# A hybrid decoder step on one core: sample tile as a fifth chain beside the prompt tiles' inversion, its transposed inverse by transposes, modulation slots by contraction step

## Chip, cores and metric

The kernel runs on one core of one Trainium2 chip. The metric is the device time of one execution in microseconds (us). In the profile PE is TensorE's matmuls, PEld its weight loads, DVE is VectorE, ACT is ScalarE, POOL is GpSimd and SP is SyncE, which issues the weight loads.

## What is computed

Two decoder layers work on 256 prompt tokens and on 64 sample tokens (8 sequences of 8). Each layer has a token mixer with four gated-linear-attention heads and four gated-delta heads, then a feed-forward (dense in layer 0, 8 experts of which 2 are used in layer 1). Shift, scale and gate of every normalization come from the conditioning, by a product with `w_ada`. The part that the change touches, for the gated-delta heads, in the reference's words:

```python
m = jnp.where(strict, beta_h[..., :, None] * kk * lmask, 0.0)
t_inv = lax.linalg.triangular_solve(eye + m, eye, left_side=True, lower=True, unit_diagonal=True)
u = t_inv @ (v * beta);  w = t_inv @ (k * beta * exp(gam));  a_qk = (q @ k.T) * lmask
# per chunk, with the state s
v_new = uu - ww @ s
o = qd @ s + aa @ v_new
s = s * exp(gl) + kd.T @ v_new
# and for every block of w_ada
mod = cs @ w_ada[l] + b_ada[l]
```

Here a chunk is a whole tile. For the samples each sequence has a state of its own, read from memory and written back. All of it is fp32; the large weight products are split into a high and a low fp32r part and take three matmuls.

## The kernel before, in words

**Tiles.** `TILES` (line 65) are prompt tokens 0 to 127 (tile 0), 128 to 255 (tile 1) and the 64 sample tokens (tile 2). A layer is: input projection (29 units of 128 outputs), mixing stage, out-projection (8 units), feed-forward. In the mixing stage five engines have each their own program, and the order of the work is written out by hand on each; semaphores counted by name and value (`after`, `PER_LAYER`) tie them together. There is no planner.

**Mixing stage, TensorE's order** (from line 910 on): scores and values of the linear-attention heads (`gla_scores`, `gla_values`) and, for the delta heads, `turn` (transposes of q, k, v to token rows, and the decay sums along rows), `turn_back` (normalized q, k transposed back) and `products` (k k and k q), for tile 0 and then tile 1. Then `invert((0, 1), ...)`, then `keys`, `new_values`, `outputs` for tile 0 and tile 1, and only then `turn`, `turn_back`, `products`, `invert`, `keys`, `new_values`, `outputs` for tile 2. VectorE's `normalize` and `strict` make the matrices of a tile (lines 1841 to 1892), ScalarE's `squares_qk`, `masks`, `turned_back`, `row_decay` stand between.

**Inversion** (lines 806, 1388 and 1894). The unit triangular matrix of a head is inverted by doubling blocks: 7 levels for a prompt tile, 3 for the sample tile, whose sequences have 8 tokens. `DM` is the matrix, `DMB` its part that belongs to a level (VectorE's `masked`, line 1839), `DT` and `DU` the inverse and its transpose so far. At each level TensorE computes DY from DMB and DU, ScalarE copies DY from PSUM, TensorE computes DT-times-DY and DY-times-DT, and VectorE subtracts one from DU (line 1914) and the other from DT (line 1913). At level 0 the first product is one with the identity. Two heads of a tile form a chain with a PSUM bank of its own; tiles 0 and 1 together make four chains whose steps alternate, tile 2 later makes two. Beside the levels stand the sample tokens of the linear-attention heads (`samples_beside`): on TensorE `gla_sample_values` at levels 1 and 2 and `gla_sample_state` at levels 3 to 6, on VectorE `spread` (line 1808), `decayed` (line 1813) and `added` (line 1819). `gla_sample_state(2)` waits for the first `added`, as they use the same two banks.

**Buffers.** The parts of tiles 0 and 1 have a set of nine buffers each (`DSET`, in the area of the split weights); tile 2 uses tile 0's set again, after tile 0 and 1 are done. `settled` holds TensorE back until VectorE and ScalarE have read a tile's results.

**Modulation.** A group `x` of `ada` is 16 output blocks: 8 contraction steps `k` of four matmuls, which write 32 rows each of one bank. SyncE loads it into 8 of the ring's 8 slots (1 MB each), in load order with all other weights; a slot is loaded again when its user has counted it done (`used`). Slot g of a half holds output quarter g for four steps k, so step 0 waits for four slots, and they come free together after step 3. In each layer three groups are computed in the mixing stage, split over TensorE's queue by `ada(x, ...)`. `ada_rows` (ScalarE), `ada_turn` (TensorE, line 648) and `ada_add` (VectorE, line 1661) finish one.

**Tail.** After `outputs(2)`: VectorE squares the heads (`heads_square`, line 1622), TensorE sums them (`heads_sum`), VectorE and ScalarE take the reciprocal root (`heads_root`, lines 1627 and 1577 to 1579, `rsqrt_seed`), TensorE spreads it over the partitions (`heads_spread`), VectorE scales (`heads_scale`, line 1639), and ScalarE and VectorE split the result into `hh` and `hl`, which the out-projection reads block by block. Weights are split by ScalarE (`high.to`, line 413) and VectorE (`low.to`, line 418).

All matmuls of the mixing stage go through the helper `mm`, line 594; all activations through line 1227.

## Time and profile before

| | |
|---|---|
| runs | 2052.96, 2054.32, 2056.16 us; median 2054.32 |
| profiled execution | 2056.35 us, its span 2054.2 us |
| PE / PEld busy | 1913.9 us (93%) / 1575.9 us (77%) |
| DVE / ACT / POOL busy | 1466.7 us (71%) / 1092.8 us (53%) / 12.6 us (1%) |
| mean granted TensorE clock | 0.956 of 2.4 GHz |
| memory read / written | 494.88 MB / 8.72 MB, 245 GB/s over the span |

The span is the time from the first to the last instruction, and the execution's own time is 2.15 us longer. Busy shares are means over stages with different limits: the experts of layer 1 (from about 960 us on) hold most of TensorE's time. The clock has two levels, 1.2 and 2.4 GHz; a value between 0.5 and 1 for a stretch says for how much of it the full one was granted. In the timeline a row merges instructions of one kind that follow each other: its first number is the start, the second the time from the first start to the last end.

### The profile page before, as it was taken

The page shows a single profiled execution, that of the slowest core. Times are in us where ns is not written, and L with a number is a line of the kernel's source. Part 1 is how long each engine was busy: PE and PEld are TensorE (multiplying, and loading weights), DVE is VectorE, ACT ScalarE, POOL GpSimd, SP SyncE. Part 2 cuts the span into 40 slices and gives each one's busy share as a digit, 9 for nine tenths or more (in the row PEclk, how much of TensorE's full clock was granted, in tenths as well). Part 3 has the DMA queues.
Part 4 walks back from the last instruction along what each step waited for, and adds up shares of the span by engine and source line. Part 5 has one row for each costly group of instructions (what it writes and reads, how often), then busy time and mean ns, then how long its engine had stood idle before and what let it go on. Part 6 is the DMA issues. An engine that isn't in the chain of part 4 may idle for free.

```text
span 2054.2 us, 25480 instructions
## 1 busy us (share of the span) xinstructions
PE 1913.9 (93%) x10376; PEld 1575.9 (77%) x10376; DVE 1466.7 (71%) x1831; ACT 1092.8 (53%) x1105; POOL 12.6 (1%) x27
## 2 busy tenths in 40 slices
PE   6997889899999989896999999999999999999995
PEld 3994757899989957565778788787787877878783
DVE  3847746654448668466688888888887888878885
ACT  3744223333337542233667676666766766767672
POOL 0000000000000000000000000000000000000000
PEclk9998999999999989797899999999999999999998
DMA  9444264343352442552699899898898998989980
GB/s 383 145 147 183 87 251 159 138 155 112 127 195 103 147 158 102 222 204 83 255 338 360 321 342 349 322 361 322 342 352 322 357 334 333 350 319 358 335 340 27
DMA packets 70616, 505.30 MB, mean 246 GB/s; under 512 B 8064, under 2 KB 8224, under 8 KB 11872
## 3 DMA queue, kind: packets, MB, share of 16 engines
q1 hardware_dynamic: 68112, 488.29, 63.4%
q0 software_dynamic: 2384, 15.34, 2.0%
q8 instruction: 84, 1.38, 0.3%
q14 instruction: 36, 0.29, 0.0%
HBM read 494.88 MB, written 8.72 MB: 245 GB/s over the span
## 4 chain that ended last, share of the span: by engine, by line
issue 55%; PE 31%; DVE 10%; ACT 2%; DMA 1%; SPq 0%; POOL 0%; DVEq 0%; ACTq 0%; POOLq 0%
PE bank L594 30%; DVE wlo L418 1%; DVE work L1687 1%; ACT L1227 1%; DMA raw<-in_ada 1%; ACT work L1227 1%; DVE work L1688 1%; DMA raw<-in_w_in 0%; DVE wscr L1839 0%; ACT wscr L1227 0%; DVE hT L1601 0%; DVE work L1782 0%; DVE wscr L1908 0%; DVE rt L1577 0%; DVE rs L1579 0%
## 5 line engine op out<-in xcount | busy, mean ns | idle before, releaser
L418 DVE TENSOR_TENSOR wlo<-raw,whi 128x2048 fp32r<-128x2048 f32 (+1 forms) x412 | 920.0, 2262 | 212.0 <-ACT whi L413 210.3
L413 ACT ACTIVATE whi<-raw 128x2048 fp32r<-128x2048 f32 (+1 forms) x412 | 761.6, 1889 | 87.4 <-PE bank L594 74.9
L594 PE MATMUL bank<-whi,hg_high 128*128 128x512 f32 x896 | 369.2, 412 | 1.5 <-DVE hg_low L2104 1.5
L594 PE MATMUL bank<-whi,hg_low 128*128 128x512 f32 x896 | 355.2, 396 | 0.0
L594 PE MATMUL bank<-wlo,hg_high 128*128 128x512 f32 x896 | 355.1, 396 | 0.0
L594 PE MATMUL bank<-hh,whi 128*128 128x320 f32 x944 | 299.7, 317 | 23.0 <-DVE hl L1609 18.6
L594 PE MATMUL bank<-hh,wlo 128*128 128x320 f32 x944 | 294.3, 312 | 0.0
L594 PE MATMUL bank<-hl,whi 128*128 128x320 f32 x944 | 294.2, 312 | 0.0
L1227 ACT ACTIVATE work<-bank 128x512 f32<-128x512 f32 (+2 forms) x209 | 97.3, 487 | 274.2 <-PE bank L594 250.6
L594 PEld LDWEIGHTS bank<-hh,whi 128*128 128x128 f32 x944 | 180.7, 191 | 30.6 <-issue 23.7
L594 PEld LDWEIGHTS bank<-whi,hg_high 128*128 128x128 f32 x896 | 169.1, 189 | 43.2 <-issue 4.4
L594 PEld LDWEIGHTS bank<-whi,hg_low 128*128 128x128 f32 x896 | 169.1, 189 | 41.1
L594 PEld LDWEIGHTS bank<-wlo,hg_high 128*128 128x128 f32 x896 | 169.4, 189 | 38.2
L594 PE MATMUL bank<-whi,act_high 128*128 128x512 f32 x448 | 185.2, 413 | 1.5 <-DVE act_low L2107 1.5
L594 PEld LDWEIGHTS bank<-hh,wlo 128*128 128x128 f32 x944 | 181.0, 192 | 0.8
L594 PEld LDWEIGHTS bank<-hl,whi 128*128 128x128 f32 x944 | 180.4, 191 | 0.0
L594 PE MATMUL bank<-wlo,act_high 128*128 128x512 f32 x448 | 177.2, 395 | 0.0
L594 PE MATMUL bank<-whi,act_low 128*128 128x512 f32 x448 | 177.1, 395 | 0.0
L594 PE MATMUL bank<-work 128*128 128x128 f32 (+9 forms) x704 | 112.6, 332 | 7.8 <-DVE work L1782 4.1
L1227 ACT ACTIVATE wscr<-bank 128x256 f32<-128x256 f32 (+3 forms) x86 | 36.9, 436 | 142.8 <-PE bank L594 112.1
L594 PEld LDWEIGHTS bank<-wscr 128*128 128x128 f32 (+2 forms) x752 | 87.9, 194 | 25.1 <-issue 15.0
L594 PE MATMUL bank<-wscr 128*128 128x128 f32 (+3 forms) x752 | 97.5, 284 | 8.5 <-DVE wscr L1908 5.8
(243 smaller groups left out, 1895.9 us busy)
## 6 DMA issues: line engine op xcount, KB each, us to landing
raw<-in_moe SPq DMA_DIRECT2D x336, 1024.0 KB, 4.8
raw<-in_ada SPq DMA_DIRECT2D x56, 1024.0 KB, 7.0
raw<-in_w_in SPq DMA_DIRECT2D x30, 1024.0 KB, 4.9
raw<-in_gu SPq DMA_DIRECT2D x22, 1024.0 KB, 4.9
raw<-in_down SPq DMA_DIRECT2D x16, 704.0 KB, 4.0
raw<-in_w_out SPq DMA_DIRECT2D x8, 1024.0 KB, 7.9
work<-in_s_gdn POOLq DMA_DIRECT2D x2, 2048.0 KB, 9.5
out_gdn_s<-work POOLq DMA_DIRECT2D x2, 2048.0 KB, 7.4
```

What stands on the lines that cost most here:

```text
L413: ac.activation(whi[:, part(n), 0:width(n)], raw[:, n % SLOTS, 0:width(n)], ACT.Copy).then_inc(S("w_high"), 1)
L418: ve.tensor_tensor(wlo[:, n % SLOTS, 0:width(n)], raw[:, n % SLOTS, 0:width(n)], whi[:, part(n), 0:width(n)], ALU.subtract).then_inc(S("w_ ...
L594: return pe.matmul(out, lhsT, rhs, start=start, stop=stop, **k)
L1227: return ac.activation(out, in_, func, **k)
L1687: go(stt(yp, XP[:, s, j:j + TP], wc[:, c, j:j + 1], yp, ALU.mult, ALU.add))
L1688: do(stt(ys, xs[:, :, j:j + LSEQ], wc[:, c, j:j + 1], ys, ALU.mult, ALU.add))
```

## The change

- Tile 2 gets a buffer set of its own (made of free parts of the two areas and of buffers that tiles 0 and 1 have done with), and goes through `turn`, `turn_back`, `products`, `normalize` and `strict` before the inversion. It is inverted as a fifth chain, of all four heads, in levels 2 to 4 of the one `invert`.
- `DT` is no longer updated. From a chain's level 2 on TensorE transposes DU (`pe.transpose`, against the identity) into the first half of the bank, computes DY into the second half, and ScalarE copies both halves in one activation (`DTY`). VectorE subtracts from DU alone. The product with the identity at level 0 becomes a transpose.
- `gla_sample_values` and the score masking of tile 2 move before the inversion, `gla_sample_state` to levels 1 to 4, and with them `spread`, `decayed` and `added`. The end of modulation group x (`ada_rows`, `ada_turn`, `ada_add`), all of group x + 1's products and the head sums of the linear-attention heads move into the inversion.
- Behind the inversion the tiles' `keys`, `new_values` and `outputs` interleave; `settled` becomes single waits. `sample_rows` goes before `second_state`. The new values get buffers `DVN`.
- The second of the first two out-projection splits goes behind the sample outputs on ScalarE, and behind `low_parts` on VectorE. The root's table load goes before the copy of the modulation rows, and the third modulation turn goes behind the spread.
- A modulation slot holds one contraction step of all four quarters: 2 KB pieces from memory, a wait, a use count and a release per step.

The diff, cut to its core (indentation shortened; bodies that it replaces are the functions printed above):

```diff
 DSP = v3(w(512, NH * NK), NH)
-DSET = [[wscr[:, at + 512 * i:at + 512 * (i + 1)] for i in range(9)] for at in (PARTS * HALF - 9 * 512, 0)]
-DY = DSET[0][7]
+DSET = [[wscr[:, at + 512 * i:at + 512 * (i + 1)] for i in (0, 1, 2, 3, 4, 5, 7, 6, 8)] for at in (PARTS * HALF - 9 * 512, 0)]
+DTY = [v3(wscr[:, at + 512 * 5:at + 512 * 7], 2) for at in (PARTS * HALF - 9 * 512, 0)]
+AT2, DU2 = R1 + 4736 - 256, DSET[1][8]
+DT2, DY2, DX2 = w(AT2, 512), w(AT2 + 512, 256), w(R1, 256)
+DSET.append([wscr[:, 9 * 512:10 * 512], wscr[:, 10 * 512:11 * 512], DSET[0][8], DT2[:, 256:], DU2[:, 256:], DT2, DU2, DY2, DX2])
+DTY.append(v3(w(AT2, 1024), 2))
+DVN = [DSET[0][7], DSET[1][7], DSET[0][5]]
+DY = DVN[2]
 D01, D34 = w(0, 512), w(2 * TL, 512)
 WQ_AT = (WORK, WORK + NSEQ * P)
 NB, XB = (B[0], B[4], B[2], B[3]), (B[5], B[6], B[7])
-IBANK = (NB[0:2], NB[2:4], NB[0:2])
+IBANK = (NB[0:2], NB[2:4], XB[1:2])
 SBANK = ((B[3], B[4]), (B[1], B[2]))
 STATE_AT = (0, 1, 3, 4)
...
     if x is not None:
-        return S("ada_mm"), 2 * x + (n - AT_ADA[x]) // 4 + 1
+        return S("ada_mm"), n + 1 - AT_ADA[x] + KD * x
...
+def chains(v):
+    yield from ((i, hs, v) for i in range(2) for hs in range(2))
+    if 2 <= v < 2 + LEVELS[2]:
+        yield 2, 0, v - 2
+def chain(i, hs):
+    nt = TILES[i][1]
+    heads = (2 * hs, 2 * hs + 1) if i < 2 else range(NH)
+    return nt, heads, slice(heads[0] * nt, (heads[-1] + 1) * nt), IBANK[i][hs]
+LEVELS = (7, 7, 3)
+STEPS = [x for v in range(7) for x in chains(v)]
...
             sp.wait_ge(*used(n - SLOTS))
-        sp.dma_start(raw[:, n % SLOTS, 0:width(n)], src).then_inc(landed[n % SLOTS], 16)
+        dst = raw[:, n % SLOTS, 0:width(n)]
+        sp.dma_start(dst if group_of(n) is None else v3(dst, 4), src).then_inc(landed[n % SLOTS], 16)
     def load_ada(x, b):
-        for g in range(4):
-            load(AT_ADA[x] + 4 * b + g, A["ada"][2 * (4 * x + g) + b, :, :])
+        for k in range(4):
+            chunks = A["ada"][8 * x + b:8 * x + 8:2, :, k * CH:(k + 1) * CH]
+            load(AT_ADA[x] + 4 * b + k, chunks.rearrange("g p c -> p g c"))
     load_ada(0, 0)
...
         for k in ks:
-            b = k // 4
+            n = AT_ADA[x] + k
             if k == 0 and x:
                 pe.wait_ge(S("ada_done"), x)
+            pe.wait_ge(landed[n % SLOTS], 16 * (n // SLOTS + 1))
             for g in range(4):
-                n = AT_ADA[x] + 4 * b + g
-                if k % 4 == 0:
-                    pe.wait_ge(landed[n % SLOTS], 16 * (n // SLOTS + 1))
                 ins = mm(ABANK[32 * g:32 * g + 32, :], small[:, k * NC_:k * NC_ + 32],
-                         raw[:, n % SLOTS, (k % 4) * CH:(k % 4 + 1) * CH], k == 0, k == KD - 1)
-            if k % 4 == 3:
-                ins.then_inc(S("ada_mm"), 1)
+                         raw[:, n % SLOTS, g * CH:(g + 1) * CH], k == 0, k == KD - 1)
+            ins.then_inc(S("ada_mm"), 1)
     def ada_turn(x):
...
+        def invert(beside):
+            after(pe, "dat", l, 3)
+            after(pe, "drowe", l, 3)
+            for v in range(LEVELS[0]):
+                for i, hs, x in chains(v):
+                    nt, heads, _, bank = chain(i, hs)
+                    DMB, DU = DSET[i][4], DSET[i][6]
+                    after(pe, "dmb", l, AT_MASK[i, hs, x])
+                    if x:
+                        after(pe, "dtu", l, AT_LEVEL[i, hs, x - 1])
+                    elif i == 2:
+                        after(pe, "gla_o", l, 3)
+                    for h in heads if x > 1 else ():
+                        o = (h - heads[0]) * nt
+                        pe.transpose(bank[0:nt, o:o + nt], DU[0:nt, h * nt:(h + 1) * nt], ident[0:nt, 0:nt])
+                    for h in heads:
+                        c = slice(h * nt, (h + 1) * nt)
+                        o = 256 + (h - heads[0]) * nt
+                        if x:
+                            ins = mm(bank[0:nt, o:o + nt], DMB[0:nt, c], DU[0:nt, c])
+                        else:
+                            ins = pe.transpose(bank[0:nt, o:o + nt], DMB[0:nt, c], ident[0:nt, 0:nt])
+                    ins.then_inc(S("dy_mm"), 1)
+                for i, hs, x in chains(v):
+                    if x == 0:
+                        continue
+                    nt, heads, _, bank = chain(i, hs)
+                    DT, DY = DSET[i][5], DSET[i][7]
+                    after(pe, "dy", l, AT_UPDATE[i, hs, x])
+                    for h in heads:
+                        c = slice(h * nt, (h + 1) * nt)
+                        o = (h - heads[0]) * nt
+                        ins = mm(bank[0:nt, o:o + nt], DT[0:nt, c], DY[0:nt, c])
+                    ins.then_inc(S("dtu_mm"), 1)
                 beside(v)
...
+            after(pe, "dtu", l, len(STEPS))
...
                 if i == 2:
-                    if h == 0:
-                        ada(x + 2, 4, 5)
                     after(pe, "dwm", l, h + 1)
...
+        def beside(v):
+            if 0 < v < 5:
+                gla_sample_state(v - 1)
+            if v == 1:
+                ada_turn(x)
+            if v > 1:
+                ada(x + 1, *((0,), (1, 2), (3, 4), (5, 6), (7,))[v - 2])
+            if v == 5:
+                after(pe, "gla_sstate", l, 2)
+                heads_sum(("heads", 2 * l + 1), QK)
         gla_scores(0)
...
+        ada(x, 5)
+        turn(2)
+        gla_sample_values(0)
+        gla_sample_values(1)
+        ada(x, 6)
+        turn_back(2)
         ada(x, 7)
-        invert((0, 1), samples_beside)
-        ada_turn(x)
+        products(2)
+        invert(beside)
         keys(0)
-        heads_sum(("heads", 2 * l + 1), QK)
         new_values(0)
-        ada(x + 1, 0, 1)
+        keys(1)
         outputs(0)
-        ada(x + 1, 2)
-        settled(0)
-        keys(1)
+        ada_turn(x + 1)
         heads_spread(("heads", 2 * l + 1))
+        after(pe, "gdn_state", l, 1)
         new_values(1)
-        ada(x + 1, 3, 4)
+        ada(x + 2, 0)
+        keys(2)
+        ada(x + 2, 1)
+        after(pe, "do", l, 1)
         outputs(1)
-        ada(x + 1, 5)
-        settled(1)
-        turn(2)
-        ada(x + 1, 6, 7)
-        turn_back(2)
-        products(2)
-        ada_turn(x + 1)
-        invert((2,), lambda v: None)
-        ada(x + 2, 0, 1, 2, 3)
-        keys(2)
+        ada(x + 2, 2, 3)
         new_values(2)
+        ada(x + 2, 4)
+        after(pe, "do", l, 2)
         outputs(2)
-        ada(x + 2, 6, 7)
+        ada(x + 2, 5)
         after(pe, "do", l, 3)
         heads_sum(("heads", 2 * l + 2), w(4 * TL, TL))
+        ada(x + 2, 6, 7)
+        heads_spread(("heads", 2 * l + 2))
         ada_turn(x + 2)
-        heads_spread(("heads", 2 * l + 2))
...
-            nt, DM, DMB = TILES[i][1], DSET[i % 2][3], DSET[i % 2][4]
+            nt, (DM, DMB) = TILES[i][1], DSET[i][3:5] if i < 2 else DSET[i][5:7]
             for b, dst in ((0, DM), (1, DMB)):
                 after(ac, "dtr", l, 3 * i + b + 1)
-                if i == 2 and b == 0:
-                    after(ac, "gdn_state", l, i)
+                if i == 2 and b == 1:
+                    after(ac, "dqd", l, i)
                 act(dst[0:nt, :], NB[b][0:nt, :], ACT.Square).then_inc(S("dsq"), 1)
             rsqrt_seed(("qk", 3 * l + i + 1), rv8[0:nt, :], rs8[0:nt, :])
...
+        def invert(beside):
+            for v in range(LEVELS[0]):
+                for i, hs, x in chains(v):
+                    if x == 0:
+                        continue
+                    nt, _, c, bank = chain(i, hs)
+                    after(ac, "dy_mm", l, AT_LEVEL[i, hs, x])
+                    if x > 1:
+                        ins = act(DTY[i][0:nt, :, c], v3(bank, 2)[0:nt, :, 0:256], ACT.Copy)
+                    else:
+                        ins = act(DSET[i][7][0:nt, c], bank[0:nt, 256:512], ACT.Copy)
+                    ins.then_inc(S("dy"), 1)
                 beside(v)
...
             act(DMB[:, 0:n4], NB[0][:, 0:n4], ACT.Copy, scale=-1.0).then_inc(S("dw"), 1)
         def new_values(i):
             after(ac, "dvn_mm", l, i + 1)
-            act(DSET[i % 2][7], NB[1][:, :], ACT.Copy).then_inc(S("dvn"), 1)
+            act(DVN[i], NB[1][:, :], ACT.Copy).then_inc(S("dvn"), 1)
         def outputs(i):
...
+        squares_qk(2)
+        gla_result(2)
+        masks(2)
+        turned_back(2)
+        row_decay(2)
+        invert(lambda v: ada_rows(x) if v == 0 else None)
+        rsqrt_seed(("heads", 2 * l + 1))
         keys(0)
         new_values(0)
-        rsqrt_seed(("heads", 2 * l + 1))
+        ada_rows(x + 1)
+        keys(1)
         outputs(0)
-        keys(1)
         new_values(1)
+        keys(2)
         outputs(1)
-        squares_qk(2)
-        masks(2)
-        ada_rows(x + 1)
-        turned_back(2)
-        row_decay(2)
-        invert((2,), lambda v: None)
-        keys(2)
-        high.to(AT_OUT[l] + 1)
+        after(ac, "ds_mm", l, 2)
+        high.to(AT_OUT[l])
         new_values(2)
         outputs(2)
+        high.to(AT_OUT[l] + 1)
         after(ac, "gla_fin", l, 1)
         for k in range(GH):
             act(hh[:, k, :], hT[:, k, :], ACT.Copy).then_inc(S("hh"), 1)
+        rsqrt_seed(("heads", 2 * l + 2))
         ada_rows(x + 2)
-        rsqrt_seed(("heads", 2 * l + 2))
...
+            if i == 2:
                 do(cp(v3(gEL[:, :], 4), v3(DX[:, 0:n4], 4)[:, :, LSEQ - 1:TS:LSEQ]))
...
+                    (nt, heads, c, bank), DU = chain(i, hs), DSET[i][6]
+                    if x + 1 < LEVELS[i]:
+                        masked(i, hs, x + 1)
+                    if x == 0:
+                        nh = len(heads)
+                        after(ve, "dy_mm", l, AT_LEVEL[i, hs, 0])
+                        do(tt(v3(DU[0:nt, c], nh), mid(ident[0:nt, 0:nt], nh),
+                              v3(bank[0:nt, 256:512], nh), ALU.subtract), "dtu")
+                        continue
+                    after(ve, "dtu_mm", l, AT_UPDATE[i, hs, x])
+                    do(tt(DU[0:nt, c], DU[0:nt, c], bank[0:nt, 0:256], ALU.subtract), "dtu")
                 beside(v)
...
             for h in range(NH):
-                ins = stt(DSP[:, h, :], DSP[:, h, :], gEL[:, 4 + h:5 + h], NB[3][:, h * P:(h + 1) * P], ALU.mult, ALU.add)
+                ins = stt(DSP[:, h, :], DSP[:, h, :], gX[:, h:h + 1], NB[3][:, h * P:(h + 1) * P], ALU.mult, ALU.add)
                 go(ins) if h < NH - 1 else do(ins, "gdn_state")
         def sample_rows():
-            t0, DMB, n4 = TP, DSET[0][4], 4 * TS
+            t0, DMB, n4 = TP, DSET[2][4], 4 * TS
             after(ve, "gla_out", l, 48)
...
+        o1, tag1 = hT[:, 0:GH, :], ("heads", 2 * l + 1)
+        def beside(v):
+            if v == 3:
                 added(0)
...
+            if v < 4:
+                spread(v)
+            if v == 1:
+                ada_add(x)
+            if v in (2, 3):
+                decayed(v - 2)
+            if v == 5:
                 added(1)
+                heads_square(tag1, o1, QK)
         arguments(1)
         gla_scored(0)
...
         gla_carried(1)
         operands(2)
         strict(1)
...
+        gla_scored(2)
         normalize(2)
         strict(2)
+        after(ve, "gla_o", l, 3)
+        invert(beside)
+        heads_root(tag1)
+        heads_gate(o1, G1, col(f"glan{l}"))
+        first_state()
         ada_add(x + 1)
...
+        heads_scale(tag1, o1, "gla_fin", False)
         sample_rows()
...
+        second_state()
+        low.to(AT_OUT[l])
         after(ve, "do", l, 3)
         def sample_values(h):
...
         o2, tag2 = hT[:, GH:, :], ("heads", 2 * l + 2)
         heads_square(tag2, o2, w(4 * TL, TL))
         low_parts(3 * l + 1, "hl_out", range(GH))
```

## Rows read from the trace of the kernel before

**Rows 1.** Stretches: us, busy PE, PEld, DVE, ACT, POOL; granted clock, DMA share, GB/s.
```profile
153.10:199.70 46.60, 36.11 (x297) 22.25 (x298) 35.51 (x94) 22.15 (x42) 1.62 (x3) 0.85 0.40 153
199.70:242.70 43.00, 40.48 (x329) 36.46 (x330) 35.33 (x82) 9.61 (x25) 0.54 (x1) 1.00 0.24 100
242.70:311.10 68.40, 55.59 (x412) 36.22 (x412) 31.02 (x72) 16.33 (x28) 1.60 (x3) 0.90 0.57 227
311.10:325.90 14.80, 11.43 (x52) 6.71 (x51) 9.53 (x20) 5.96 (x13) 0.00 (x0) 0.67 0.68 261
729.20:902.30 173.10, 145.66 (x1082) 103.92 (x1082) 111.08 (x266) 53.42 (x107) 3.52 (x7) 0.86 0.45 178
```

**Rows 2.** Timeline of the inversion: sample values, a sample-state product, a level of products.
```profile
207.57 2.30 PE L594 MATMUL bank<-work 128*128 128x64 f32 x20
...
222.85 1.07 PE L594 MATMUL bank<-work 32*64 32x512 f32 x4
...
223.85 5.43 PEld L594 LDWEIGHTS bank<-wscr 128*128 128x128 f32 x48 [0.81 <-issue]
```

**Rows 3.** Timeline: the twelve transposes of one turn.
```profile
177.85 1.29 PEld L779 LDWEIGHTS bank<-cf,work 128*128 128x128 f32 x12 [2.04 <-DVE work L1879]
```

**Rows 4.** Groups by form, 199.7 to 242.7: count | busy us, mean ns | idle before.
```profile
L1839 DVE TENSOR_TENSOR wscr<-wscr,cb 128x256 f32<-128x256 f32 x24 | 10.2, 425 | 1.8 <-PE bank L594 1.0
...
L1227 ACT ACTIVATE wscr<-bank 128x256 f32<-128x256 f32 x24 | 9.2, 384 | 28.0 <-PE bank L594 27.3
L1913 DVE TENSOR_TENSOR wscr<-wscr,bank 128x256 f32<-128x256 f32 x20 | 8.4, 421 | 4.7 <-PE bank L594 4.1
...
L1813 DVE TENSOR_TENSOR work<-work,gla_expend 128x1024 f32<-128x1024 f32 x2 | 2.5, 1226 | 0.1
...
L1819 DVE TENSOR_TENSOR work<-work,bank 128x512 f32<-128x512 f32 x2 | 1.3, 684 | 0.0
```

**Rows 5.** Timeline after the inversion: spread, two modulation steps, sample values and outputs.
```profile
260.41 2.33 PE L594 MATMUL bank<-rs,cf 128*128 128x320 f32 x10
...
264.45 1.92 PE L594 MATMUL bank<-raw,small 128*32 128x512 f32 x16
...
297.91 2.05 PE L594 MATMUL bank<-work 128*128 128x128 f32 x16
...
307.38 0.60 ACT L1227 ACTIVATE wscr<-bank 128x512 f32<-128x512 f32 x1 [3.06 <-PE bank L594]
308.03 0.29 PEld L594 LDWEIGHTS bank<-work,wscr 64*128 64x128 f32 x2 [0.93 <-ACT wscr L1227]
```

**Rows 6.** Timeline of the tail, and the two low splits ahead of it.
```profile
302.91 4.49 DVE L418 TENSOR_TENSOR wlo<-raw,whi 128x2048 fp32r<-128x2048 f32 x2
...
311.09 3.41 PE L594 MATMUL bank<-raw,small 128*32 128x512 f32 x16
...
315.19 1.28 ACT L1227 ACT_TABLE_LOAD   x1
...
316.59 0.45 ACT L1227 ACTIVATE rs<-rv 128x320 f32<-128x320 f32 x1
...
318.94 4.63 PE L594 MATMUL bank<-rs,cf 128*128 128x320 f32 x10 [3.06 <-DVE rt L1629]
```

**Rows 7.** Timeline: first and last of tile 2's preparation on VectorE, 24 instructions.
```profile
272.32 0.68 DVE L1848 TENSOR_REDUCE rv<-wscr 64x4 f32<-64x512 f32 x1
...
281.91 0.17 DVE L1892 COPY g_expend<-wscr 128x32 f32<-128x32 f32 x1
```

**Rows 8.** Two stretches, columns as in rows 1.
```profile
273.00:282.00 9.00, 5.40 (x53) 3.09 (x52) 8.45 (x23) 3.85 (x8) 0.00 (x0) 1.00 1.01 411
282.00:293.00 11.00, 8.89 (x60) 5.61 (x64) 5.64 (x17) 1.08 (x4) 0.00 (x0) 0.56 0.54 229
```

**Rows 9.** Timeline of the start: first projection split and modulation add.
```profile
32.67 1.91 ACT L413 ACTIVATE whi<-raw 128x2048 fp32r<-128x2048 f32 x1 [4.54 <-DMA raw<-in_w_in]
...
36.89 0.30 DVE L1661 TENSOR_TENSOR mod<-bank,small 128x144 f32<-128x144 f32 x1
```

168 lines of the change are left out of this document (40 added, 128 removed).

## Prediction

> **What bounds the kernel now.** I first cut the first layer's mixing stage into stretches by busy time [rows 1]. The reader should see 172.8 us from 153.1 to 325.9, with TensorE busy 143.6 (36.1 + 40.5 + 55.6 + 11.4) and its granted clock under 1.00 in three of the four stretches. The second layer repeats it (173.1 us). So this stage, twice, is where TensorE waits or runs at 1.2 GHz. Outside it the change touches only the load and use order of the modulation weights. Inside it the bound changes hands. From 153.1 to 199.7 VectorE prepares the two prompt tiles. From 199.7 to 242.7 their four inversion chains keep TensorE busy 40.5 of 43.0 us, at full clock. From 242.7 to 311.1 one tile after another goes round TensorE, ScalarE and VectorE, and 12.8 us are idle on TensorE. 311.1 to 325.9 is the tail, a chain through all three engines before the out-projection can use its fifth input block.
>
> **Prices.** In the inversion a 128-wide product is two instructions of 0.113 us (5.43 / 48), so 0.23 [rows 2]; a transpose is one of 0.107 us (1.29 / 12) [rows 3]. Four heads make 0.9 or 0.45. VectorE pays 0.42 for a mask and 0.42 for a subtraction, ScalarE 0.38 for a copy of two heads, and the sample work beside costs VectorE 1.23 (decay) and 1.28 (two rows of state add) [rows 4]. The sample-state product costs TensorE 1.07 and one contraction step of the modulation 0.96 at full clock (1.92 / 2) and 1.7 at half (3.41 / 2) [rows 2, 5, 6].
>
> **Term 1, inversion starts later: +11.7 us a layer.** Tile 2's preparation moves ahead of the inversion. On VectorE it runs from 272.32 to 282.08, so 9.8 us [rows 7]. The sample scores' masking (a memset and two small products, estimate 0.8, by the 0.28 to 0.42 of other 64- and 128-row operations of a few hundred columns) leaves level 0 and joins it. TensorE must now do turn, both sample-value calls (2.3 each [rows 2]), three modulation steps and turn-back in that time, and ScalarE does a table load and one result copy before the masks. By my count the key products come 1.9 late for VectorE. Against that, the two modulation steps that stood in front of turn-back of tile 1 are gone, which gives 0.6 (tile 1's products then hang on the operands of the sample scores). Sum 9.8 + 0.8 + 1.9 - 0.6 = 11.9, less 0.2 for two wide masks in place of four narrow ones.
>
> **Term 2, inversion itself: +6.0 and +3.0.** The second operand's update, two products (0.45) and one VectorE subtraction (0.42) a chain and level, becomes two transposes (0.21) and a wider copy. That copy is not in the trace: bounds are 0.38 (no more than one copy) and 0.77 (two), I take 0.6, and ScalarE, busy 9.6 of 43, hides either. A chain then costs TensorE 0.45 + 0.21 + 0.45 = 1.11 and VectorE 0.9, four chains 4.4 and 3.6. Level 0's products with the identity become transposes too, under VectorE's masks. On top lie tile 2's chain in levels 2 to 4 (64-wide, 12 instructions a level or fewer, 0.3, 1.0 and 1.3), a state product in levels 1 to 4 and eight modulation steps of the next group. By level, in TensorE's time: 0 and 1 together 7.5 (VectorE paces level 0, then state product and turn); level 2, 4.4 + 0.3 + 1.0 + 0.9 = 6.6; level 3, 5.4, then a **new wait**: the third state product may not overwrite its bank before VectorE's first state add, which now stands in the same level behind five chains' subtractions, 3.7 us late, then 1.0 + 1.8, so 11.9; level 4, 4.4 + 1.3 + 1.0 + 1.8 = 8.5; level 5, 4.4 + 1.8, then a **second wait** of 3.2 us, because the head sums stand in TensorE's queue before level 6 and need VectorE's second state add (1.28) and the squares (1.5), then 0.7, so 10.1; level 6, 4.4. Sum 49.0 against 43.0. The clock adds: level 0 and tile 2's products are thin work for TensorE, and in the trace the stretch 273 to 282, busy 5.4 of 9.0, is followed by one at 0.56 [rows 8]. I count half clock over part of levels 1 and 2, +3.0 (bounds 0 and 7, the work of those levels).
>
> The Trainium skill speaks against this part: TensorE: Matmul & The Clock Gate, Part 4: PE-mode transpose, says that transposes do not count as TensorE work for keeping the clock up. This trace does not separate it; it is taken up as a rival below.
>
> **Term 3, from the end of the inversion to the end of the sample outputs: -37.4.** Now 68.4 us [rows 1], of which tile 2's preparation and inversion (270.5 to 289.3) and eight of its fourteen modulation steps leave, some of them at half clock. What remains for TensorE at full clock: keys of three tiles and two tiles' values (1.0 + 3 x 0.88 + 1.75), outputs 0 and 1 (1.75 + 2.65), the turn 0.45, the spread 2.3 [rows 5], sample values 307.38 - 297.91 = 9.4 and sample outputs 311.09 - 308.03 = 3.1 [rows 5, 6], six modulation steps at 0.86 start to start, 5.2, and 0.8 waiting for a ScalarE copy. Sum 31.0. The ScalarE copies that TensorE waited for lie under modulation steps and the next tile's keys; without that cover each costs some 0.8. The sample rows on VectorE (two memsets, 2.4) are ready before the sample values begin, since TensorE needs 14 us to get there. The buffers for the new values and the decay column moved to a free tile take waits away that nothing hung on; I price them, the dropped settle calls and the shifted state copy at 0. The state load (2 MB) is issued after the fourth state product, over 15 us before its use.
>
> **Term 4, the tail: +2.2.** Today 14.8 us. The second out-projection split leaves its place under the sample values for a place behind the last outputs: 1.9 on ScalarE before the copies of the head blocks and 2.24 on VectorE before the root [rows 6]. ScalarE's reciprocal-root table, today loaded from 315.19 on, with the root at 316.59, is loaded before it is needed; the variance is there at about 315.7, which gives 0.9; and the modulation steps no longer delay the head sums, 1.2. The turn of the third modulation group now stands behind the spread, and VectorE's scale waits for it, 1.3. I leave the spread at half clock (4.63 against 2.33 [rows 5, 6]), since TensorE has 5 us of nothing before it. Sum 1.9 + 2.2 - 0.9 - 1.2 + 1.3, less 1.1 where the two splits overlap: 2.2.
>
> **Term 5, modulation slots by contraction step: 0.** At the start TensorE can multiply when one slot is there, not four, and after the last load one step remains instead of four. But ScalarE's copy of the rows stands behind the split of the first projection weights, which waited for its load until 32.67 and ended at 34.58, and the modulation add follows VectorE's half of that split at 36.89 [rows 9]. Both hang on the load order, which stays. Each load now fetches pieces of 2 KB in place of 8 KB. No row shows it; below 0 is excluded by the splits, above I allow +5 at the start (8 MB at a quarter less speed) and take 0. In the layers the loads have slack.
>
> **Sum.** 11.7 + 6.0 + 3.0 - 37.4 + 2.2 = -14.5 a layer, -29 in all. What follows the stage (feed-forward, experts) only shifts. The profiled execution took 2056.35 us (span 2054.2 and 2.15 around it): 2027.3. The median shown is 2.0 lower, so **2025**. A measurement of this kernel can tell about 0.2%, 4 us, from no change.
>
> **Rivals.**
> *Waits shorter, clock kept (2015).* TensorE's full clock through levels 1 and 2 and the spread, and the two new waits half as long: 3.0 + 2.3 + 3.5 less than forecast, some -23 a layer, 2009; half of that gives 2015 to 2017. For it: 204 to 243 ran at 1.00. Against: the idle is placed as in the stretches that fell. Chance 0.20.
> *The chains bind on VectorE or on hand-overs (2039).* My sum passes over some 60 hand-overs between engines in the inversion; at 0.1 us each and a late sample-value call it loses 7 more a layer. Chance 0.12.
> *Half clock through the inversion (slower).* Place: levels 2 to 6. They hold 33 us of TensorE work a layer; at 1.2 GHz each of these costs one more, less the 7 of new waits that they fill and the 3 counted: +23 a layer, so 2025 + 46 = 2071. It decides from 14.5 us of such work a layer on. For it: TensorE's work is thinner per level and broken by two waits of over 3 us; a stretch at 5.4 of 9.0 busy lost the clock [rows 8]. Against: levels 3 to 5 are 70 to 100% busy between the waits, as 199.7 to 242.7 was. Chance 0.05, and 0.05 for half of it (2048).
> The skill's rule on transposes, named above, would make this rival likelier than the rows do, since a fifth of each level's TensorE time is transposes.
> *Loads of 2 KB pieces slow (2045).* Twice the time for the first 8 loads adds some 20 us at the start. Nothing in the trace speaks for it. Chance 0.03.
> My own forecast, 2015 to 2037: 0.55.
>
> **How the numbers follow.** Range 2008 to 2043: it holds the forecast, the faster rival and the hand-over one, and leaves out 0.13 and some of the edges. Faster by over 0.2%: all but the slower rival and a little of the mild ones, 0.93; slower 0.05; the same 0.02.
>
> **What would show it.** VectorE's first level-0 mask of the last chain set near 211 in place of 199.7; the last level's products ending near 263; no product reading the second operand as moving data in the inversion; TensorE idle over 3 us before the third state product and before the first head sums; sample outputs ending near 294; the out-projection's fifth block near 311 in place of 325.9. I am wrong if the inversion takes over 60 us, if the granted clock there is near 0.5, or if the first projection product starts later than at 41.

## The result and the profile after

The changed kernel takes **2042.7 us** (median of 4 runs, 2042.4 to 2043.3) against 2055.2 us of the kernel before on the same chip (4 runs, 2053.0 to 2056.7). The ratio is 0.9938, 95% interval 0.9925 to 0.9950. So it is faster, by 12.5 us and not by the 29 forecast. The profiled execution took 2043.25 us, its span 2041.5. PE busy is 1903.1 us (before 1913.9), DVE 1450.5 (1466.7), ACT 1101.1 (1092.8).

The stretches of layer 0 that answer to [rows 1] (columns as there; the last row is the stage of layer 1):

```profile
154.13:216.19 62.06, 50.46 (x370) 34.09 (x371) 45.18 (x118) 28.25 (x53) 1.43 (x3) 0.75 0.50 170
216.19:270.40 54.21, 47.33 (x362) 33.99 (x360) 33.01 (x68) 15.51 (x27) 1.60 (x3) 0.91 0.47 163
270.40:302.48 32.08, 31.39 (x240) 23.92 (x239) 13.39 (x31) 7.75 (x13) 0.55 (x1) 1.00 0.66 250
302.48:319.10 16.62, 11.23 (x59) 6.01 (x58) 11.59 (x21) 6.31 (x13) 0.00 (x0) 0.79 0.59 223
722.10:887.20 165.10, 139.16 (x1027) 97.52 (x1027) 103.26 (x237) 57.91 (x105) 3.57 (x7) 0.87 0.53 188
```

The preparation became 62.1 us (from 46.1, counted from VectorE's first operation of the stage), the inversion 54.2 (43.0), what follows it 32.1 (68.4), the tail 16.6 (14.8). The stage of layer 1 went from 173.1 to 165.1. A gain of some 8 us a layer stands where 14.5 were forecast, and it is the first two stretches that are too long. Their granted clocks, 0.75 and 0.91, say where to look. TensorE's timeline of the changed kernel through tile 2's preparation:

```profile
202.07 5.51 PE L610 MATMUL bank<-work 128*128 128x64 f32 x40
207.51 1.94 PE L610 MATMUL bank<-raw,small 128*32 128x512 f32 x8
209.38 0.69 PE L806 MATMUL bank<-cf,work 64*128 64x64 f32 x4
209.86 0.63 PE L806 MATMUL bank<-cf,wscr 64*128 64x64 f32 x4
210.42 1.93 PE L610 MATMUL bank<-raw,small 128*32 128x512 f32 x8
212.28 1.97 PE L610 MATMUL bank<-work 128*64 128x64 f32 x16
```

and VectorE's, of the same stretch:

```profile
208.32 0.68 DVE L1886 TENSOR_TENSOR wscr<-bank,g_beta 64x512 f32<-64x512 f32 x1
213.51 0.42 DVE L1895 TENSOR_TENSOR work<-bank,work 64x256 f32<-64x256 f32 x1 [4.51 <-PE bank L610]
```

The two modulation steps around turn-back take 1.94 and 1.93 us, the time of half clock (1.06 at full), and so do the key products (1.97, against 1.15 in the kernel before). VectorE waits 4.5 us for them. Three stretches with their granted clocks (columns as in rows 1), the first at tile 1's key products, the others at tile 2's preparation:

```profile
191.00:198.00 7.00, 6.10 (x34) 4.86 (x38) 3.03 (x10) 0.97 (x2) 1.09 (x2) 0.50 0.30 94
200.00:205.00 5.00, 4.94 (x44) 4.61 (x42) 4.63 (x13) 2.88 (x5) 0.00 (x0) 1.00 0.67 213
206.00:214.00 8.00, 8.00 (x48) 4.52 (x47) 3.39 (x7) 3.16 (x6) 0.00 (x0) 0.50 0.40 135
```

The kernel before has 0.98 where the first row has 0.50:

```profile
191.00:198.00 7.00, 5.37 (x50) 3.77 (x47) 4.02 (x11) 2.51 (x6) 1.08 (x2) 0.98 0.30 101
```

The third row deserves a second look: TensorE was busy 4.94 of the 5 us in the second row and went on without a pause, and still the clock is at half from 206 on. No idle gap stands in front of this fall, and no run shows what causes it. TensorE's timeline further on, at the two waits that the prediction placed:

```profile
236.33 0.67 PE L610 MATMUL bank<-work 64*64 64x64 f32 x8
240.70 1.97 PE L610 MATMUL bank<-work 32*64 32x512 f32 x4 [3.69 <-DVE work L1838]
242.60 3.64 PE L610 MATMUL bank<-raw,small 128*32 128x512 f32 x16
...
265.13 0.75 PE L610 MATMUL bank<-work,cf 128*32 128x320 f32 x8 [3.07 <-DVE work L1641]
```

Both are there, 3.7 and 3.1 us long (forecast 3.7 and 3.2). Behind the first the clock is at half: the state product takes 1.97 instead of the 1.07 of [rows 2], two modulation steps 3.64 instead of 1.92. Behind the second it stays full. The tail, whose rows answer to [rows 6]:

```profile
306.84 2.28 DVE L424 TENSOR_TENSOR wlo<-raw,whi 128x2048 fp32r<-128x2048 f32 x1
309.05 0.48 DVE L1646 TENSOR_SCALAR rv<-bank 128x320 f32<-128x320 f32 x1
...
311.92 3.86 PE L610 MATMUL bank<-rs,cf 128*128 128x320 f32 x10 [3.17 <-DVE rt L1648]
```

The first row is VectorE's half of the second out-projection split. It stands in front of the variance (the second row), which the root and then TensorE's spread (the third) wait for.

**Given back behind the layers.** When the out-projection of layer 1 reaches its fifth block, the changed kernel is 15.5 us ahead (887.16 against 902.64), and at the last scatter product still 15.05 (2006.38 against 2021.43). Another 2.3 us go in one place, VectorE's first operation after the experts. The kernel before, and then the changed one:

```profile
2029.00 0.48 DVE L1644 SCALAR_TENSOR_TENSOR xT<-hT,mod,xT 128x256 f32<-128x256 f32 x1 [1.54 <-issue]
```

```profile
2016.26 0.48 DVE L1663 SCALAR_TENSOR_TENSOR xT<-hT,mod,xT 128x256 f32<-128x256 f32 x1 [3.85 <-issue]
```

Nothing in the data holds it (the last scatter add has ended 3.85 us earlier, and "issue" is named), and the DMA queues carry nothing but instruction packets in this time. It is where VectorE's program jumps from the experts to what follows them.

### The profile page after: what moved, and what is told of

Its sections match the earlier page's. It is cut to its first block, busy times and chain, and to the rows that moved or that the text cites. A ratio compares the mean times of both kernels' runs of the same rounds, so it can differ in the third digit from the quotient of the medians.

```text
span 2041.5 us, 25178 instructions
## 1 busy us (share of the span) xinstructions
PE 1903.1 (93%) x10264; PEld 1566.4 (77%) x10264; DVE 1450.5 (71%) x1771; ACT 1101.1 (54%) x1101; POOL 12.7 (1%) x27
## 4 chain that ended last, share of the span: by engine, by line
issue 56%; PE 30%; DVE 11%; ACT 2%; SPq 1%; DMA 1%; POOL 0%; DVEq 0%; ACTq 0%; POOLq 0%
PE bank L610 29%; DVE wlo L424 2%; DVE work L1706 1%; SPq L524 1%; DMA raw<-in_w_in 1%; ACT L1241 1%; DVE wscr L1858 1%; PE bank L834 1%; DVE work L1707 1%; ACT work L1241 1%; DVE wscr L1930 0%; ACT whi L419 0%; DVE hT L1620 0%; DVE hl L1628 0%; DVE work L1838 0%
## 5 line engine op out<-in xcount | busy, mean ns | idle before, releaser
L1241 ACT ACTIVATE work<-bank 128x512 f32<-128x512 f32 (+3 forms) x217 | 101.3, 487 | 277.4 <-PE bank L610 247.9
L610 PE MATMUL bank<-work 128*128 128x128 f32 (+10 forms) x736 | 123.1, 344 | 13.4 <-DVE work L1838 7.4
L610 PEld LDWEIGHTS bank<-work 128*128 128x128 f32 (+4 forms) x736 | 83.6, 188 | 38.5 <-issue 19.7
L1241 ACT ACTIVATE wscr<-bank 128x512 f32<-128x512 f32 (+2 forms) x74 | 41.5, 567 | 132.7 <-PE bank L610 107.9
L610 PEld LDWEIGHTS bank<-whi,act_high 128*128 128x128 f32 x448 | 84.3, 188 | 24.9 <-issue 4.3
## 6 DMA issues: line engine op xcount, KB each, us to landing
work<-in_s_gdn POOLq DMA_DIRECT2D x2, 2048.0 KB, 12.6
out_gdn_s<-work POOLq DMA_DIRECT2D x2, 2048.0 KB, 7.4
```

The source lines that it names most:

```text
L610: return pe.matmul(out, lhsT, rhs, start=start, stop=stop, **k)
L1241: return ac.activation(out, in_, func, **k)
```

## The experiments

All edits are against the changed kernel unless said otherwise. The runs stem from several chips, on which the kernel before took 2054.4 to 2055.9 us, and their medians are compared with the 2043.4 of e0_after. Beside the medians I use one length from each trace, from VectorE's first operation of the mixing stage of layer 0 to that of layer 1 (the row that waits 13.5 us for ScalarE). It leaves out the start of the kernel, which scattered: in these traces the stage of layer 0 begins anywhere between 151.0 and 156.0. **Layer length**: before 575.6 us, changed kernel 568.0 and, in its second trace (e0_after), 567.3, to which the other lengths are compared.

**e0_after**, no edit.

> The changed kernel again, as the base for the others of this chip: 2042 to 2044 us in every theory. Two theories on the last 2.3 us (the start of the final residual on VectorE follows the last scatter 3.85 us later in the changed kernel, 1.54 in the kernel before, with 'issue' as the releaser and only instruction packets in the DMA queues): if it belongs to where the code lies, it is 3.8 again here; if it is chance, it scatters between 1.5 and 4.

Measured: 2043.4 us (2042.7 to 2044.5), the wait again 3.83. It belongs to the program. In this trace tile 2's key products ran at full clock (1.15 us) and VectorE still waited 4.17 for them, since the sample value calls (5.80) and the first modulation step (1.94) ahead of them did not.

**e1_add0**, the wait in level 3.

```diff
-                    if v == 3:
-                        added(0)
                     if v < 4:
                         spread(v)
...
                         decayed(v - 2)
+                    if v == 2:
+                        added(0)
```

> VectorE's first sample state add goes to the end of level 2, one level ahead of TensorE's third state product. Theory A (the wait of 3.7 us in level 3 is on the path and it also costs the clock behind it): the wait goes, the state product and two modulation steps behind it run at full clock (2.8 instead of 5.6), VectorE pays its 1.28 in level 2 instead: 4 to 5 us a layer, 2033 to 2035. Theory B (VectorE paces the levels anyway, the wait only shows it): the wait turns up in front of level 3's products and the time stays within 1 us a layer, 2041 to 2043.

Measured: 2035.0 us (2031.2 to 2036.6), layer length 561.4. Theory A. The same 12 us in the repeated changed kernel and in this one (columns as in rows 1):

```profile
237.00:249.00 12.00, 8.31 (x47) 3.50 (x47) 6.83 (x13) 0.48 (x1) 0.54 (x1) 0.72 0.27 91
```

```profile
237.00:249.00 12.00, 12.00 (x107) 7.92 (x100) 7.29 (x16) 3.23 (x6) 0.00 (x0) 1.00 0.55 187
```

The hole is closed, and the clock stays full. (The stage began 2.9 us earlier in the second trace, so the two windows do not hold quite the same work.) A wait of 3.7 us had cost 4.2 a layer by the medians and 5.9 by the layer length, whose trace is of the fastest of the four runs.

**e2_sums**, the wait before the head sums.

```diff
-                    if v == 5:
+                    if v == 6:
                         after(pe, "gla_sstate", l, 2)
                         heads_sum(("heads", 2 * l + 1), QK)
...
-                    if v == 5:
+                    if v == 4:
                         added(1)
+                    if v == 5:
                         heads_square(tag1, o1, QK)
```

> The head sums of the linear-attention heads go from ahead of level 6 to behind it on TensorE, and VectorE's second state add from level 5 to level 4. Theory A (the 3.1 us in which TensorE waits before the head sums are on the path): level 6 starts at once, its copies and products run under VectorE's squares, 2.5 to 3 us a layer less, 2037 to 2038. Theory B (level 6 has to wait for VectorE's level 5 anyway): under 1 us a layer, 2041 to 2043.

Measured: 2037.9 us (2036.5 to 2038.5), layer length 565.4. Theory A, 2.8 us a layer by the medians, 2.0 by the layer length. The clock had stayed full behind this wait, and it cost no more than its length.

**e7_tail**, the splits.

```diff
-                high.to(AT_OUT[l])
+                high.to(AT_OUT[l] + 1)
                 new_values(2)
                 outputs(2)
-                high.to(AT_OUT[l] + 1)
...
-                low.to(AT_OUT[l])
+                low.to(AT_OUT[l] + 1)
                 after(ve, "do", l, 3)
...
-                low.to(AT_OUT[l] + 1)
                 heads_root(tag2)
```

> Both out-projection splits stand again ahead of the sample outputs, on ScalarE before the new values of tile 2 and on VectorE before its wait for the outputs, both of which have over 5 us of idle time there. Theory A (VectorE's split of 2.28 us is on the path from the head sums to the root): the root starts 2.2 us earlier a layer, 2038 to 2040. Theory B (the split fills VectorE's wait for the head sums, which come late by the two modulation steps): under 0.5 us a layer, 2042 to 2044.

Measured: 2034.1 us (2033.7 to 2035.6): 9.3 us less, twice what Theory A gave. The timeline of its tail:

```profile
304.16 3.16 PE L610 MATMUL bank<-raw,small 128*32 128x512 f32 x16
304.66 0.48 DVE L1645 TENSOR_SCALAR rv<-bank 128x320 f32<-128x320 f32 x1
...
307.54 2.43 PE L610 MATMUL bank<-rs,cf 128*128 128x320 f32 x10 [0.22 <-DVE rt L1647]
```

The root starts right behind the head sums, which is the 2.3 us. And TensorE comes to the spread from the modulation steps without a pause, 0.22 us in place of 3.17, so that the spread takes 2.43 us and not 3.86. The two make 3.7 us a layer; the layer length is 564.3, 3.0 less, and the median gives 4.6.

**e4_fill** tests that second half by itself.

```diff
                 ada(x + 2, 6, 7)
+                for _ in range(12):
+                    mm(NB[0][:, 0:P], ident, ident)
                 heads_spread(("heads", 2 * l + 2))
```

> Twelve idle products of ident with ident (2.8 us at full clock), which compute nothing that is used, stand between the last two modulation steps and the spread of the tail, where TensorE has 3.2 us of idle time. Theory A (the spread takes 3.87 instead of some 2.3 us because the engine stood idle in front of it): the spread falls to 2.3 to 2.6, and as much of the time: 1 to 1.6 us a layer, 2040 to 2042. Theory B (the low clock there is the late effect of the gap from 304.8 to 305.9 or of the mixed work before): the spread stays at 3.9 and the time the same, 2043.

Measured: 2040.5 us (2039.4 to 2041.3). The tail of its trace:

```profile
308.02 2.94 PE L610 MATMUL bank<-cf 128*128 128x128 f32 x24
312.91 2.43 PE L610 MATMUL bank<-rs,cf 128*128 128x320 f32 x10 [1.94 <-DVE rt L1650]
```

Products that compute nothing make the work behind them faster, by 1.4 us a layer here, as much as the median fell. Theory A. In front of the spread stand 1.9 us of idle time here, 3.2 in the changed kernel. The head sums and modulation steps ahead of the fill happened to run at full clock in this trace. They did so in e1_add0 and e2_sums too, where without a fill 4.8 us of idle time follow and the spread takes 4.03 and 4.00, so it is the fill that helps.

**e6_notr**, the transposes undone.

```diff
-                            for h in heads if x > 1 else ():
...
-                                pe.transpose(bank[0:nt, o:o + nt], DU[0:nt, h * nt:(h + 1) * nt], ident[0:nt, 0:nt])
...
                                 ins = mm(bank[0:nt, o:o + nt], DT[0:nt, c], DY[0:nt, c])
+                            for h in heads if x < LEVELS[i] - 1 else ():
...
+                                ins = mm(bank[0:nt, o:o + nt], DY[0:nt, c], DT[0:nt, c])
...
+                            if x < LEVELS[i] - 1:
+                                go(tt(DT[0:nt, c], DT[0:nt, c], bank[0:nt, 256:512], ALU.subtract))
                             do(tt(DU[0:nt, c], DU[0:nt, c], bank[0:nt, 0:256], ALU.subtract), "dtu")
```

> The transposes of levels 2 to 6 are undone: the second operand is updated again by a product and a VectorE subtraction, all else stays. Theory A (prices by instruction): TensorE pays 21 chain updates of 0.45 and saves 22 sets of transposes of 0.21, VectorE pays 21 subtractions of 0.42, of which some fills its idle time: inversion 4.5 to 8 us longer a layer, 2051 to 2059. Theory B (transposes cost the clock, as TensorE: Matmul & The Clock Gate of the Trainium skill has it): the stretch at 0.50 in level 3 and the low clock at the head of the inversion go, worth 3 or more, and the net is 1.5 to 5 us a layer, 2045 to 2053, with a granted clock of 1.00 from level 1 to the end.

Measured: 2054.1 us (2051.8 to 2057.5, 11 runs), ratio to before 0.9994 (0.9985 to 1.0003), layer length 575.9. Theory A. That is the layer of the kernel before: **without the transposes the rest of the change, tile 2's chain beside the others included, brings nothing**. Whether the transposes would bring as much without the rest, no run shows. TensorE's timeline in its level 3 and before its head sums:

```profile
244.91 1.97 PE L610 MATMUL bank<-work 32*64 32x512 f32 x4 [3.54 <-DVE work L1836]
246.81 3.64 PE L610 MATMUL bank<-raw,small 128*32 128x512 f32 x16
...
270.79 1.14 PE L610 MATMUL bank<-work,cf 128*32 128x320 f32 x8 [3.06 <-DVE work L1639]
```

Wait and half clock are there without these transposes (those of level 0 stay), and the head sums, which took 0.75 in the changed kernel, run mostly at half clock (1.14). The granted clock of its inversion is 0.89 (216.4 to 276.0) where the changed kernel has 0.91. So these runs show no part of the clock's fall that is owed to the transposes of levels 2 to 6; the rule of the Trainium skill that the prediction names (TensorE: Matmul & The Clock Gate, Part 4: PE-mode transpose) would have had it rise.

**e3b_prep and e3c_prep**, the order of tile 2's preparation.

```diff
                 turn(2)
                 gla_sample_values(0)
-                gla_sample_values(1)
-                ada(x, 6)
                 turn_back(2)
-                ada(x, 7)
                 products(2)
+                gla_sample_values(1)
+                ada(x, 6)
                 invert(beside)
```

(cut: also step 7 beside level 0, ScalarE's result copy behind the row decay, and VectorE's wait for it in level 5)

> The preparation of tile 2 gets another order on TensorE: turn, first sample value call, turn back, key products, second sample value call, modulation step 6; step 7 goes beside level 0; ScalarE's result copy goes behind the row decay, and VectorE's wait for it to level 5. Theory A (the 4.5 us in which VectorE waits for tile 2's key products come from what stands ahead of turn-back and products in TensorE's queue, not from their own length): VectorE's wait falls under 1 us, and the inversion starts 3 to 4 us earlier a layer, 2035 to 2037. Theory B (the late stretch at half clock is what delays it, whatever the order): the wait falls by less than 2 us, and what stood there is paid at level 0, 2041 to 2044.

```diff
-                ada(x, 5)
                 turn(2)
                 gla_sample_values(0)
+                ada(x, 5)
                 gla_sample_values(1)
-                ada(x, 6)
                 turn_back(2)
-                ada(x, 7)
                 products(2)
+                ada(x, 6, 7)
```

> The preparation of tile 2 again, after the other order brought nothing: modulation step 5 goes between the two sample value calls, steps 6 and 7 behind the key products, all ahead of the inversion as in the changed kernel. Theory A (a modulation step at half clock in front of turn-back and one in front of the products make VectorE wait; behind the products they fall into TensorE's wait for the last decay): VectorE's wait of 4.5 us falls to 1 or 2 and the inversion starts 2 to 3 us earlier, 2037 to 2040. Theory B (the stretch at half clock from the sample values on sets when the inversion can start, in whatever order): the inversion starts within 1 us of where it did, 2042 to 2045.

Measured: 2048.0 (2045.3 to 2048.6) and 2050.4 us (2048.3 to 2054.6), layer lengths 572.1 and 574.7. Both made it worse, which neither theory had. TensorE's timeline of e3b_prep:

```profile
207.48 6.35 PE L610 MATMUL bank<-work 128*64 128x64 f32 x36 [0.47 <-ACT work L1242]
213.76 1.94 PE L610 MATMUL bank<-raw,small 128*32 128x512 f32 x8
215.63 1.97 PE L841 MATMUL bank<-cf,wscr 128*128 128x128 f32 x8
```

VectorE's wait for tile 2's products is gone (0.52 us), but TensorE, at half clock from 205 on, is not free for level 0 before 215.6: the second sample value call, in the first row with the products, now takes some 4.4 us where it takes 2.3 at full clock. VectorE then waits 5.07 us for level 0. In e3c_prep a gap of 1.57 us opens before the turn, which with the second sample value call runs at half clock (2.74 for 12 transposes, 4.45 for the call); the late call also holds up ScalarE's masks, and VectorE waits 7.05 us. In the changed kernel, with step 5 in front of the turn and both calls behind it, the turn (1.47) and most of the two calls (5.51 for both) ran at full clock.

**e5_slots**, the modulation slots as before (the diff's four edits on slots and use counts taken back).

> The modulation slots are undone alone: a slot holds one output quarter for four contraction steps again, is fetched in pieces of 8 KB and comes free with three others after step 3. Theory A (this part changes nothing but the 0.5 us of later issues at the start): within 1.5 us of the changed kernel, 2042 to 2045, its first projection split 0.5 us earlier. Theory B (a slot that comes free after each step is what lets the loads keep up with the modulation steps packed into the inversion): TensorE waits for modulation weights in the inversion or behind it, 3 us or more a layer, over 2048.

Measured: 2041.7 us (2039.5 to 2044.4), layer length 568.4, no wait of TensorE for a load in either layer's inversion or tail; the first projection split at 32.76, 0.43 earlier than in the changed kernel. Theory A. Runs that scatter by 5 can't tell 0 from 1.7 us, but the starts of all the traces together can: the first projection product stands between 39.9 and 41.1 us in the four with the slots as before (the kernel before, this one, c4, c6; mean 40.7) and between 41.3 and 43.4 in the twelve with the new ones (mean 42.1). So the new slots cost some 1.4 us, at the start alone.

**e9_shift**, code moved by 42 VectorE instructions.

```diff
-            ve.memset(gAB[:, :], 0.0)
+            for c in range(24):
+                ve.memset(gAB[:, c:c + 1], 0.0)
...
-            ve.memset(lgE[:, :], 0.0)
+            for c in range(19):
+                ve.memset(lgE[:, c:c + 1], 0.0)
+            ve.memset(lgE[:, 19:24], 0.0)
```

> The only edit: at the very start two of VectorE's memsets are cut into 44 narrow ones, 42 instructions more, under its first wait for data. Theory A (the 3.85 us before the final residual is instruction fetch that depends on where the code behind the branch lies; the kernels with 60 and 42 more VectorE instructions have 1.54 there): it falls to 1.5, and the time by 2.3 us, 2040 to 2042. Theory B (it hangs on the work around it, which is unchanged): 3.85 and 2043.

Measured: 2041.4 us (2040.2 to 2042.0), and the row is

```profile
2013.22 0.48 DVE L1663 SCALAR_TENSOR_TENSOR xT<-hT,mod,xT 128x256 f32<-128x256 f32 x1 [1.54 <-issue]
```

Theory A. e6_notr, with as many instructions more, has 1.54 too, and every other version with the 1771 VectorE instructions of the changed kernel 3.8 to 4.1.

**Together.** c2 is e1_add0, e2_sums and e7_tail in one.

> The three edits that brought time, together: first state add in level 2, second in level 4, head sums behind level 6, both splits ahead of the sample outputs. If they are independent, their gains add, 8.4 + 5.5 + 9.3 = 23: 2020. If the first two remove the same wait of VectorE twice, or the earlier work collides with loads that arrive later, 3 to 8 us of it are missing: 2023 to 2028.

Measured: **2015.5 us** (2014.0 to 2017.2), ratio to before 0.9801 (0.9787 to 0.9814), layer length 554.7. The gains add (23.2), and 5 us more: 12.6 by the layer length, where the three alone shorten it by 5.9, 2.0 and 3.0, together 10.9. What the rest is made of stays open.

**e10_steps**, on c2:

```diff
                 turn(1)
+                ada(x, 5)
                 gla_values(1)
...
-                ada(x, 5)
+                ada(x, 6)
                 turn(2)
                 gla_sample_values(0)
                 gla_sample_values(1)
-                ada(x, 6)
                 turn_back(2)
```

> The combination of before (c2, 2015.5 us) with the modulation steps placed otherwise in the preparation: step 5 between tile 1's turn and its values, where TensorE has 1.83 us of idle time and runs at half clock behind it, step 6 ahead of tile 2's turn, none between the sample values and turn-back. Theory A (the idle gaps ahead of tile 1's values cost the clock from 184 to 200, and the queue order costs tile 2's products the rest): tile 1's value products take 3.6 to 4.4 instead of 5.4 us, VectorE's waits for the key products, 3.4 and 4.5 us, shrink by 3 or more together, 2009 to 2012. Theory B (the clock falls there whatever fills the gap, and the order only moves the wait): each wait within 1 us of what it was, 2014 to 2018.

Measured: 2012.1 us (2010.8 to 2013.9), ratio 0.9798 (0.9785 to 0.9812), layer length 552.2. The median is at the edge of Theory A, but the ratios don't part it from c2, and what Theory A asked of the waits isn't there: the first is still 3.42 us and the value products take 5.12, so the clock falls there in spite of the filler; only the second falls, from 4.17 to 2.87. Theory B has the clock right. By the layer length the order of the queue is worth 2.4 us.

**c4** is c2 with e5_slots and e9_shift, **c6** is c4 with e10_steps.

> The combination (c2, 2015.5 us) with the modulation slots undone and the 42 small VectorE instructions at the start. If both effects are real and independent, 1.7 and 2.3 to 2.6 us: 2011 to 2012. If the slots by contraction step do help once the inversion is dense, 2013 or more.

> All edits that brought time, together: c4 (2013.0 us) with the modulation steps of e10_steps. If the order of the steps brings what it brought on c2, 3.4 us: 2009 to 2010. If the slots of before, which come free four at a time, delay the loads now that step 5 and 6 are used elsewhere, 2012 or more.

Measured: 2013.0 (2010.1 to 2013.9) and 2011.3 us (2007.8 to 2012.5), ratios 0.9802 and **0.9781 (0.9768 to 0.9795)**, layer lengths 554.9 and 551.9. The layer of c4 is that of c2 (554.7), and what c4 gains lies in the jump (1.54 for 4.13) and at the start; its median, 2013.0, can't choose between the two expectations, nor can that of c6, which falls between its two. The steps' order brings 3.0 by the layer length on c4 too. c6 is the best by its trace and its ratio, though each single step from c2 to it is smaller than the runs can tell. It is 32 us faster than the changed kernel and 44.6 faster than its own runs of before.

## Why the prediction was right and wrong

The sign was right, and 2042.7 lies just inside the range (to 2043), but the gain was under half of the forecast, and the signs of being wrong that the prediction names did not point at it: the inversion took 54.2 us at a clock of 0.91, and the third, a first projection product later than 41, came up by 0.4 (41.37, in the kernel before 40.85) and concerns the start alone. The step that failed most is in Term 1: it priced TensorE's queue ahead of the inversion at full clock, and that queue ran at half. The profiled spans differ by 12.7 where the sum had 29, so 16.3 us are to be found.

- **Term 1, start of the inversion: wrong, +15.9 for +11.7.** VectorE's first level-0 mask stands at 216.19, 62.06 behind its first operation of the stage; before, 46.11. The length of the preparation on VectorE was right; what failed is "1.9 late" for the products and the 0.6 gained on tile 1. Tile 2's products came 4.5 late, since the end of the sample value calls, two modulation steps, turn-back and the products ran at half clock, and I had priced that queue at full clock. By the rows at either clock (0.9 on the calls, 0.9 on each step, 0.4 on the first half of the products) that is 3 us, more than the 2.6 that are missing. Tile 1's products came 0.8 later and not 0.6 earlier, for the same reason (the sample scores and its key products, 24 instructions, took 4.40 us for 2.43). That is 4.0 of the 4.2. The two modulation steps whose removal was to give this 0.6 had kept TensorE busy in the kernel before, and the clock was full again by 191; without them two waits of 1.2 and 0.8 us stand there, and it stays at half to about 199. No run puts them back, so that link is argued and not shown, and why the clock falls a second time near 206, in dense work, is open. e3b_prep and e3c_prep show that two other orders don't buy the time back, e10_steps that some of it can be had.
- **Term 2, the inversion: 54.2 for 52.** Both new waits were where and as long as forecast, and e1_add0 and e2_sums show that both are on the path. Missing was that the clock is at half behind the first: 0.9 on the state product and 1.7 on two modulation steps, 2.6 us. That the total is only 2.2 off is partly luck. By the rows the levels took 7.7 (0 and 1), 7.1, 15.2, 9.4, 10.3 and 4.6 us, where the prediction had 7.5, 6.6, 11.9, 8.5, 10.1 and 4.4 and then added 3.0 for half clock in levels 1 and 2. These ran at full clock, so the 3.0 was not paid there, and it hid the 3.3 that level 3 took too long. The wide copy takes 0.60 (mean of 20), as priced.
- **Term 3: 32.1 for 31.0**, and **term 4: 16.6 for 17.0**, right, by way of the row prices. But e7_tail shows that the tail's price need not be paid: put where both engines were idle, the splits give back 3.0 us a layer by the layer length, 4.6 by the medians. The text had this cost as given by the change, and rightly, yet the half clock of the spread, which it "left", hangs on the same split.
- **Term 5, slots: 0**, small but not nothing. In the profiled pair the first split came 0.5 later, over all traces the first product 1.4 later (see e5_slots), inside the 0 to 5 that the prediction allowed.
- **What follows "only shifts": wrong by 2.7.** 2.3 us is the jump behind the experts (e9_shift). The other 0.4 goes between the out-projection and the experts' end: the counting products of the router took 3.60 us where before had 2.13, and the experts' full clock came back sooner.
- **Sum of the misses**: layer 0 made 7.6 and layer 1 8.4 instead of 14.5 each, 13.0 short; 0.5 at the start, 2.3 and 0.4 behind the layers: 16.2 of 16.3.
- **The rivals.** The nearest in time are that of the 2 KB pieces (2045), which has 1.4 us at the start where it asked for 20, and that of the hand-overs (2039), for another reason than the one that held. The faster rival's own terms (8.8 us a layer) give 2007, not 2009; it did not come. The rival of half clock through the inversion had the mechanism that did the harm, in the wrong place and size: the clock fell in the preparation and behind one wait, and levels 4 to 6 kept it (1.00 from 249 to 270). The rule on transposes that would have made it likelier is not borne out by e6_notr, which has the same two low stretches and one more. (The transposes are a fifth of the prompt chains' products, 0.21 of 1.11 us, and not of each level's TensorE time: in the whole inversion they are 21 sets, by these prices some 4.6 of 47.3 us.)

What the prediction did not see at all: which part of the change earns. It does not price the transposes apart; by the expectation of e6_notr, made after the result, they are worth 4.5 to 8 us of the 14.5, and the move of tile 2 with all else the rest, 6.5 to 10. e6_notr measures 7.9 us a layer for the transposes on top of the rest and nothing for the rest alone, whose own waits and low clock eat what it saves.

## What to carry to other kernels

Price TensorE's queue at the clock that the stretch will have: an idle gap that the change opens costs its own length, and it can cost half as much or more again on the work behind it (3.7 and 2.6 us in level 3). A piece of work that moves away may have kept the clock up for what stands behind it (Term 1, argued from the rows). A wait placed by hand in an engine's program is worth a second look at once: moving a few operations by a level and one split ahead of a wait (c2, 28 us) brought twice what the change did. When two parts of a change come together, undo each alone before saying which of them pays.

## What the runs showed of the hardware

- The price of a gap. Behind the gap of 3.7 us in level 3 and those of 3.2 and 4.8 us in the tail the work ran at half clock; behind the 1.9 us of e4_fill it did not. Behind 3.1 us before the head sums it did not in the changed kernel (0.75 us) and did in e6_notr (1.14). In the preparation it did so behind gaps of 1.2 to 1.8 us, in the kernel before as well, and from 206 on with no gap of over 0.2 us in the 12 us ahead. So in these runs the length of one gap does not tell whether the clock falls.
- The jump behind a long branch region costs VectorE 1.54 or 3.8 to 4.1 us, by the position of its code: 42 instructions more at its start moved it from the second to the first. The Trainium skill (Runtime: NRT & Kernel Launch, Instruction fetch mechanics) says that a taken branch out of the loaded pages makes the engine wait for a fetch. The traces fit this and put the two numbers on it (idle time named "issue", instruction packets alone in the queues); that the fetch fills the time is not shown by itself.
